# Stick-breaking attention: high and low weights in one output product, output gate on POOL

## What is computed

```python
z = jnp.einsum('bhqd,bhkd->bhqk', qb, kb).astype(jnp.float32) * scale
log_one_minus = jnp.where(mask, jax.nn.log_sigmoid(-z), 0.0)
suffix = lax.cumsum(log_one_minus, axis=3, reverse=True) - log_one_minus
weights = jnp.where(mask, jnp.exp(jax.nn.log_sigmoid(z) + suffix), 0.0)
outs.append(jnp.einsum('bhqk,bhkd->bhqd', weights.astype(vb.dtype), vb))
...
y_sb = jnp.einsum('bsw,wd->bsd', (o_sb * jax.nn.silu(sb_z)).astype(x.dtype), w_o_sb[layer])
```

## Time and profile before

| | |
|---|---|
| median of 3 runs | 809.24 us (808.31 to 809.7) |
| the profiled execution | 809.52 us, of it 807.8 us from first to last instruction |
| TensorE, matmul | 791.0 us busy (98%), 4441 instructions |
| DVE | 581.6 us busy (72%) |
| ACT | 410.0 us busy (51%) |
| POOL | 30.4 us busy (4%), 32 instructions |
| chain that ended last | 94% TensorE |
| granted clock | 0.999 of full speed |

### The profile page before, as it was taken

How to read it: one execution, slowest core, us unless ns; L and a number is a source line. 1 busy time by engine, 2 the same in 40 slices (tenths; PEclk the granted TensorE clock), 3 DMA queues, 4 the chain that set the end, 5 groups by cost and what they waited for, 6 DMA issues and landing times.

```text
span 807.8 us, 11845 instructions
## 1 busy us (share of the span) xinstructions
PE 791.0 (98%) x4441; PEld 662.3 (82%) x4441; DVE 581.6 (72%) x823; ACT 410.0 (51%) x706; POOL 30.4 (4%) x32
## 2 busy tenths in 40 slices
PE   5999999999999999999999999999999999999996
PEld 4778888888888888889889888888888888888885
DVE  6528997989798798956645646566457777779985
ACT  7526675666666466655244144244343343365442
POOL 1540000000000000020000000000000000000000
PEclk9999999999999999999999999999999999999999
DMA  9862112202120220021111010244443333395222
GB/s 316 277 225 53 27 28 52 52 26 52 53 51 26 53 52 27 27 80 54 30 50 27 3 52 27 79 143 152 147 131 105 105 104 105 105 360 213 105 105 104
DMA packets 72483, 76.31 MB, mean 94 GB/s; under 512 B 3804, under 2 KB 57207, under 8 KB 71928
## 3 DMA queue, kind: packets, MB, share of 16 engines
q1 hardware_dynamic: 72386, 75.71, 29.5%
q10 hardware_dynamic: 54, 0.01, 0.0%
HBM read 55.79 MB, written 15.73 MB: 89 GB/s over the span
## 4 chain that ended last, share of the span: by engine, by line
PE 94%; ACT 2%; DVE 1%; DMA 1%; issue 1%; SPq 0%; DVEq 0%; ACTq 0%
PE pj L698 29%; PE tr L1002 5%; PE sc L950 5%; PE ob L950 5%; PE ob L790 5%; PE pj L842 4%; PE ob L1002 4%; PE pj L1002 4%; PE tr L800 4%; PE sc L1002 3%; PE pj L714 3%; PE pj L823 3%; PE tr L1060 2%; PE sc L767 2%; PE sc L766 2%; PE pj L1060 2%
## 5 line engine op out<-in xcount | busy, mean ns | idle before, releaser
L698 PE MATMUL pj<-h_hi,w_lo 128*128 128x512 f32 x336 | 134.2, 399 | 0.0
L698 PE MATMUL pj<-h_hi,w_hi 128*128 128x512 f32 x336 | 133.9, 398 | 0.0
L698 PE MATMUL pj<-h_lo,w_hi 128*128 128x512 f32 x336 | 133.8, 398 | 0.0
L1671 DVE TENSOR_TENSOR_SCAN surv<-surv 128x128 f32<-128x128 f32 (+3 forms) x64 | 86.5, 1351 | 16.3 <-ACT beta L1169 15.9
L698 PEld LDWEIGHTS pj<-h_hi,w_lo 128*128 128x128 f32 x336 | 63.5, 189 | 12.1 <-issue 0.5
L698 PEld LDWEIGHTS pj<-h_lo,w_hi 128*128 128x128 f32 x336 | 63.3, 189 | 12.0 <-issue 0.3
L698 PEld LDWEIGHTS pj<-h_hi,w_hi 128*128 128x128 f32 x336 | 63.6, 189 | 11.6 <-issue 0.2
L1210 ACT ACTIVATE wt_hi<-tr 128x512 fp32r<-128x512 f32 (+2 forms) x96 | 43.6, 490 | 37.8 <-PE tr L800 36.3
L1594 DVE TENSOR_TENSOR w_lo<-w_raw,w_hi 128x1024 fp32r<-128x1024 f32 x33 | 40.3, 1222 | 27.0 <-ACT w_hi L1102 26.7
L1703 DVE TENSOR_TENSOR wt_lo<-tr,wt_hi 128x512 fp32r<-128x512 f32 (+2 forms) x96 | 50.2, 550 | 7.9 <-ACT wt_hi L1210 7.4
L1674 DVE TENSOR_TENSOR beta<-beta,surv 128x128 f32<-128x128 f32 (+3 forms) x64 | 48.6, 759 | 2.2
(11 more groups left out here) (400 smaller groups left out, 1910.3 us busy)
## 6 DMA issues: line engine op xcount, KB each, us to landing
w_raw<-in_w_in SPq DMA_DIRECT2D x30, 512.0 KB, 3.8
y_scratch<-y_ring SPq DMA_DIRECT2D x28, 256.0 KB, 2.0
graw<-in_w_in SPq DMA_DIRECT2D x14, 512.0 KB, 5.2
y_back<-y_scratch SPq DMA_DIRECT2D x14, 512.0 KB, 5.2
x_t<-in_x SPq DMA_DIRECT2D x8, 512.0 KB, 6.6
wrow<-in_w_out SPq DMA_DIRECT2D x4, 1024.0 KB, 7.2
w_scratch<-wsum SPq DMA_DIRECT2D x4, 1024.0 KB, 5.0
wout_raw<-in_w_out SPq DMA_DIRECT2D x8, 512.0 KB, 7.2
```

The lines of the kernel that those rows point to most:

```text
L698: mm = pe.matmul(pj[bank][:, :], (w_lo if p == 2 else w_hi)[:, slot, k, :], (h_lo if p == 1 else h_hi)[:, k, HALF * h:HALF * h + HALF], st ...
L1671: dve.tensor_tensor_scan(s[:, ::-1], s[:, ::-1], s[:, ::-1], 1.0, ALU.mult, ALU.bypass)\
```

## The change

`wt_hi` and `wt_lo` become the two planes of one tile `wt`, at the same places in memory. One product then moves both: 2 planes of 256 columns (of 128 in the last block), into the two halves of the bank `ob`. ACT copies and DVE adds 512 columns instead of 256. The sum of the two planes, and the multiplication by the gate, go to POOL. `o_low` becomes two tiles. New waits: ACT's copy waits for the gate multiplication of two groups before (`g_done`), and the two `z_silu` multiplications of DVE wait for POOL's multiplications of the pair before.

```diff
-        wt_hi = [at("wt_hi0", 108, [P, 6, 256], F32R), at("wt_hi1", F + 8, [P, 8, 256], F32R)]
-        wt_lo = [at("wt_lo0", 114, [P, 6, 256], F32R), at("wt_lo1", F + 16, [P, 8, 256], F32R)]
+        wt = [at("wt0", 108, [P, 2, 6, 256], F32R), at("wt1", F + 8, [P, 2, 8, 256], F32R)]
+        wt_hi, wt_lo = [w[:, 0, :, :] for w in wt], [w[:, 1, :, :] for w in wt]
-        o_low = at("o_low", 122, [P, 2, 256])
+        o_low = [at("o_low0", 122, [P, 2, 256]), at("o_low1", F + 80.25, [P, 2, 256])]
         @block.gpsimd
         def _(pool):
+            pool.sem_inc(g_done, 8)
...
-            pool.wait_ge(g_done, 8 * PAIRS)
+            def gate_output(i, gg):
+
+                e, g = gg // 4, gg % 4
+                own, qs = slice(HD * e, HD * e + HD), slice(256 * g, 256 * g + 256)
+                low = o_low[gg % 2]
+                pool.wait_ge(o_free, 8 * i + gg + 3)
+                pool.tensor_tensor(low[own, 0, :], low[own, 0, :], low[own, 1, :], ALU.add).then_inc(o_summed, 1)
+                pool.wait_ge(o_summed, 8 * i + gg + 1)
+                pool.wait_ge(proj_free, 8 * i + 7 + g // 2)
+                pool.tensor_tensor(G[own, i, qs], low[own, 0, :], z_silu[own, qs], ALU.mult).then_inc(g_done, 1)
+
+            for i in range(PAIRS):
+                for gg in range(8):
+                    gate_output(i, gg)
+
+            pool.wait_ge(g_done, 8 * PAIRS + 8)
...
                         for b in range(blocks):
                             c0 = P * max(0, b - 2 * g)
-                            for part in (wt_hi, wt_lo):
-                                mm = pe.matmul(ob[gg % 2][:, c0:256], v_st[:, e, b, :], part[g % 2][:, b, c0:256],
-                                               start=(b == 0 and part is wt_hi),
-                                               stop=(b == blocks - 1 and part is wt_lo))
+                            mm = pe.matmul(ob[gg % 2][:, :].rearrange("p (a q) -> p a q", a=2)[:, :, c0:256],
+                                           v_st[:, e, b, :], wt[g % 2][:, :, b, c0:256], start=(b == 0),
+                                           stop=(b == blocks - 1))
                         mm.then_inc(av_done, 1)
...
                         act.wait_ge(av_done, 8 * i + gg + 1)
-                        act.activation(o_low[HD * e:HD * e + HD, gg % 2, :], ob[gg % 2][HD:P, 0:256],
+                        act.wait_ge(g_done, 8 * i + gg + 7)
+                        act.activation(o_low[gg % 2][HD * e:HD * e + HD, :, :],
+                                       ob[gg % 2][HD:P, :].rearrange("p (a q) -> p a q", a=2),
                                        ACT.Copy).then_inc(o_copied, 1)
...
-            act.wait_ge(g_done, 8 * PAIRS)
+            act.wait_ge(g_done, 8 * PAIRS + 8)
...
                             dve.wait_ge(proj_act, c + 1)
+                            dve.wait_ge(g_done, 8 * i + (8 if h else 6))
...
-                        low = o_low[own, gg % 2, :]
+                        low = o_low[gg % 2][HD * e:HD * e + HD, :, :]
                         dve.wait_ge(o_copied, 8 * i + gg + 1)
-                        dve.tensor_tensor(low, ob[gg % 2][0:HD, 0:256], low, ALU.add).then_inc(o_free, 1)
-                        dve.wait_ge(o_free, 8 * i + gg + 3)
-                        dve.wait_ge(proj_free, 8 * i + 7 + g // 2)
-                        dve.tensor_tensor(G[own, bass.ds(i, 1), 256 * g:256 * g + 256].rearrange("p a c -> p (a c)"),
-                                          low, z_silu[own, 256 * g:256 * g + 256], ALU.mult).then_inc(g_done, 1)
+                        dve.tensor_tensor(low, ob[gg % 2][0:HD, :].rearrange("p (a q) -> p a q", a=2), low, ALU.add)\
+                            .then_inc(o_free, 1)
```

More of the change, by code:

```diff
@@ L342, in stickbreak_gla_hybrid @@
         o_free = sem("o_free")
+        o_summed = sem("o_summed")
         g_done = sem("g_done")
@@ L1709, in pair @@
                         e, g = gg // 4, gg % 4
-                        own = slice(HD * e, HD * e + HD)
-                        low = o_low[own, gg % 2, :]
+                        low = o_low[gg % 2][HD * e:HD * e + HD, :, :]
                         dve.wait_ge(o_copied, 8 * i + gg + 1)
-                        dve.tensor_tensor(low, ob[gg % 2][0:HD, 0:256], low, ALU.add).then_inc(o_free, 1)
-                        dve.wait_ge(o_free, 8 * i + gg + 3)
-                        dve.wait_ge(proj_free, 8 * i + 7 + g // 2)
-                        dve.tensor_tensor(G[own, bass.ds(i, 1), 256 * g:256 * g + 256].rearrange("p a c -> p (a c)"),
-                                          low, z_silu[own, 256 * g:256 * g + 256], ALU.mult).then_inc(g_done, 1)
+                        dve.tensor_tensor(low, ob[gg % 2][0:HD, :].rearrange("p (a q) -> p a q", a=2), low, ALU.add)\
+                            .then_inc(o_free, 1)
                     for j, h, k, p in plan[step]:
```

## The result

The changed kernel takes 813.37 us (median of 4 runs, 813.16 to 813.55), the kernel before in the same comparison 809.47 us. The ratio is 1.0048, with a 95% interval from 1.0036 to 1.006. That is slower by 3.9 us, inside the stated range and on the side that was forecast, 1.6 us under the 815.0 forecast.

A forecast was written before the change was run, and what follows sets the result against it. TensorE, busy 98% of the span, was taken to bound the kernel, with DVE the only engine holding it up. From 809.5 us, -2.8 (pairing) + 0.5 (stage end) + 7.8 (POOL holding DVE) gave 815.0 us; range 806 to 819.5.

The forecast's parts named there:

- TensorE's saving: Attention output products: pairing saves 0.007 us per full block and 0.06 per last block, 2.8 us less in all.
- POOL beside DVE: Attention stage: POOL's SBUF reads hold DVE, making TensorE late at tile 7/group 3 and group 5; 7.8 us more, chance 0.41.
- The price of a hold: At a held DVE instruction with two SBUF inputs: DVE waits for POOL's whole instruction, 0.72 us.
- Where POOL gets in: On DVE: POOL enters where DVE pauses for its own semaphore, between scan and `beta`, not between instructions without a wait.
- POOL at every boundary: Rival: POOL's addition also enters between `w_lo` and scan behind groups 4 and 6; 1.1 us more per pair, 819.4 us, chance 0.12.
- The cover: Distances from DVE's end to TensorE's start, 0.66 us at tile 7, 0.13 and 0.06 at groups 3 and 5, absorb lateness.
- The end of the stage: After the last output group, TensorE waits for DVE's last addition, 0.21 + 0.27 us later; 0.5 us more.
- The new wait of ACT and DVE's wait at `z_silu`: Waits on POOL multiplications of two groups or a pair earlier; both costed at nothing.
- DVE's lighter load: Per output group, DVE without the multiplication becomes 0.28 us shorter; no separate term in the sum.
- That POOL would not hold DVE up: Rival: DVE keeps its reads whatever POOL does, only POOL waits; 806.9 us, chance 0.31.
- That the scan is free: Rival: the scan's two inputs are one tile, so POOL works beneath scans and meets `beta` only behind short ones; 808.0 us, chance 0.14.
- That pairing saves nothing: Rival: the paired product costs what two products cost; adds 2.8 us to any case, chance 1 in 10.

The follow-up runs named there:

- run 5: The kernel before with only its gate multiplication moved to POOL, untimed, products unpaired; 808.61 us, ratio 0.9993.
- run 4: The changed kernel with an added `w_ready` wait on each of POOL's two instructions, so they start when DVE turns to `wt`; 806.11 us, ratio 0.9954.
- runs 4 to 7: run 4, run 5, and the changed kernel with the `w_ready` wait only on POOL's addition (808.62 us) or only on its multiplication (810.05 us).
- run 2: The kernel before with two unneeded 64x256 POOL additions reading SBUF behind each of DVE's 32 additions; 819.47 us, ratio 1.0126.
- run 1: The changed kernel with POOL's two instructions per output group replaced by memsets, which write and read nothing; 806.07 us, ratio 0.9956.

## Why the prediction was right, and which terms were off

**TensorE's saving** was forecast as 2.8 us and measured larger. The last output group of the stage in the changed kernel, TensorE's timeline:

```profile
353.56 1.86 PE L806 MATMUL ob<-wt,v_st 128*128 128x512 f32 x8
355.26 0.40 PE L715 MATMUL pj<-h_hi,w_hi 128*128 128x512 f32 x1
```

Eight blocks take 1.70 us, where the earlier trace rows had 351.43 - 349.58 = 1.85. A group of two blocks takes 0.35, so a full block costs 0.226 and a last one 0.12. The full block saves 0.0126 us, not 0.007: I had priced the paired product by projection products, and it is a little faster than they are. 128 x 0.0126 + 32 x 0.06 = 3.5 us, and by run 5 against run 4 0.9 per pair, 3.6. The estimate of 0.4 us from the page "TensorE: Matmul & The Clock Gate", section "Back-to-back issue gap", of the Trainium skill was further off. Beyond that a DVE without the multiplication gives back 0.19 us per pair (73.19 before, 73.00 in run 5), 0.8 us for four, which the sum left out: group 3 starts 0.23 us behind the product ahead, not 0.34, and its 16 products take 1.86 us, not 1.94.

**POOL beside DVE** was forecast at +7.8 us and is +8.0: 2.00 us per pair between the change and run 4. The mechanism is as written, exclusion both ways. Its parts were not, and that they add up to nearly the same is luck. From group 1 to group 3 the hold costs 0.74 us (17.43 against 16.69 between their starts), where the sum had 1.3; from 3 to 5 it costs 1.02 (15.30 against 14.28), not 0.6; 0.24 us are elsewhere, where the sum had none. Three assumptions of the sum failed.

- *The price of a hold.* DVE is not held for POOL's full 0.72 us, but for 0.36 behind a scan and 0.55 behind `w_lo`. Take the end of a held DVE instruction less its length without a hold: 161.13 + 1.45 - 1.09 = 161.49 for `beta`, and POOL's multiplication ends at 161.62, 0.13 us later. For the scan at 158.85 it is 159.07 against 159.22, for the one at 183.50 184.04 against 184.19. In the other held instructions from 130 to 206 us, of this kernel and of runs 4 to 7, it is 0.12 to 0.15 us as well. So DVE runs as if it had started 0.14 us before POOL's end, and loses what is left of POOL's instruction then. A POOL instruction that had waited ended 0.53 us behind the scan and 0.60 us behind `w_lo`, which gives the 0.36 and the 0.55.
- *Where POOL gets in.* "Not between instructions that follow without a wait" is wrong: POOL does get in there. The rival of POOL at every boundary had the entry right and its price too high.
- *The cover.* The distance of 0.66 us at tile 7 was read from the end of `beta`, but the turning there waits for the first `wt` behind it, which the earlier trace rows already named (`wt_lo`), and has no cover: 0.57 us reach TensorE (0.89 against 0.32 in run 4), and the sum had 0.4. The 0.13 and 0.06 us at groups 3 and 5 are no cover either. TensorE had waited there already, 0.34 and 0.43 us behind the product ahead, and the change has the same distances, 0.14 and 0.05: they are the time from DVE's end to TensorE's start. Nor are the four pairs alike: in the last one group 3 did not wait before.

**The end of the stage** was forecast at +0.5. TensorE, kernel before:

```profile
352.61 0.48 PE L870 MATMUL sc<-lr_p,w_up 32*128 32x256 f32 x2 [0.50 <-DVE o_low L1713]
```

And changed kernel:

```profile
355.49 0.40 PE L715 MATMUL pj<-h_lo,w_hi 128*128 128x512 f32 x1
356.91 0.48 PE L886 MATMUL sc<-lr_p,w_up 32*128 32x256 f32 x2 [1.03 <-DVE o_low L1731]
```

1.42 us from the last projection product to these, and 0.90 before (351.71 to 352.61): 0.52 us more. The new wait of ACT and DVE's wait at `z_silu` cost nothing that a trace shows.

**The rivals.** That POOL would not hold DVE up is out by `beta`'s 1.45 us and by run 2. That the scan is free is out by the scans of 2.24 and 2.03 us. That pairing saves nothing is out by 0.226 us per product.

The sum with the measured terms is -3.6 - 0.8 + 8.0 + 0.5 = +4.1 us, and the medians differ by 3.9. The forecast had +5.5, too much because both gains were larger than the sum had them: the saving by 0.8 us, and DVE's lighter load, which it put at nothing, by 0.8. POOL's term takes 0.2 of that back.

By the Trainium skill, "SBUF — State Buffer", section "Who interferes with whom", the second to come is blocked for the whole instruction. The traces agree both ways but for an edge: POOL's multiplication, 0.73 us alone, still took 0.53 us behind the end of the scan that it had met, and DVE stood until 0.12 to 0.15 us before the end of POOL's record.

## What to carry to other kernels

Work that is moved to an idle engine is not free if that engine and the busy one exclude each other: price it by what it does to the neighbours, and look first at the instructions that read SBUF twice. Its place can be worth more than the move: two waits on a semaphore that says "the neighbour now reads PSUM" turned 0.5% slower into 0.5% faster with no work taken away. Where an engine is late in few places, a hold costs only ahead of those, so read the cover place by place, and from the wait that the profile names: of the distance from a producer's end to its consumer's start, only what exceeds the distance at a place where the consumer did wait is cover.

## What the runs showed of the hardware

- POOL instructions that read SBUF and DVE instructions with two SBUF inputs exclude each other, whichever comes first. A POOL addition of 64x256, 0.73 us alone, lengthened a DVE `beta` behind a scan by 0.36 us and a scan behind `w_lo` by 0.55, in each case until 0.12 to 0.15 us before POOL's end; `wt`, with one input in PSUM, kept its 0.68 us beside it.
- A waiting POOL instruction gets in even between two DVE instructions that follow each other without a wait, `w_lo` and a scan.
- A scan whose two inputs are the same tile is held too: 2.83 us in place of 2.28.
- A product that moves two pieces of 256 columns, 6 or 8 KB apart, takes 0.226 us, no more than one of 512 neighbouring columns (0.232 in the same stage).
- POOL memsets beside DVE left DVE's durations as they were: 0.31 us each in run 1, and 1.81 us beside a subtraction of 1.23 us with two SBUF inputs.
